# Rounded activations moved by 32 to 224 bytes against the rounded weights, in a two-layer hybrid diffusion backbone

## What is computed

```
hc = ada_ffn_half(hc, ...); hx = ada_ffn_half(hx, ...)     # SwiGLU, 1024 -> 2*2816 -> 1024
uc, ux = modulate(rms_norm(h, mix_norm[l]), shift, scale)
yc, yx = token_mixing(...)   # u @ w_in -> gated MLP | delta rule | latent attention
m = sigmoid(ga)*(ya @ w_a) + sigmoid(gb)*(yb @ w_b) + sigmoid(gc)*(yc @ w_c)
h = h + gate * (m @ w_o)
h = ada_ffn_half(h, ...)     # second SwiGLU
```

## Time and profile before

| | |
|---|---|
| runs | 2534.43 and 2532.1 us, median 2533.26 |
| profiled execution, first to last instruction | 2531.9 us |
| what lies around the span | 0.2 to 2.5 us, by the two runs |
| mean granted TensorE clock | 0.987 of full speed |
| busy PE / weight load / DVE / ACT / POOL | 2430.3 / 2061.2 / 1466.0 / 945.7 / 90.4 us |
| weights and inputs read | 306.18 MB, 121 GB/s over the span |

### The profile page before, as it was taken

One profiled execution on the slowest core, in us unless ns is written; L12 is line 12 of the kernel. 1 busy time (PEld: TensorE's weight loads), 2 busy tenths in 40 slices (PEclk: granted clock), 3 DMA queues, 4 the chain that ended last, 5 costly groups with the idle time before them and its releaser, 6 DMA issues.

```text
span 2531.9 us, 37811 instructions
## 1 busy us (share of the span) xinstructions
PE 2430.3 (96%) x15806; PEld 2061.2 (81%) x15806; DVE 1466.0 (58%) x2287; ACT 945.7 (37%) x1537; POOL 90.4 (4%) x122
## 2 busy tenths in 40 slices
PE   5999999999989999999999999999999989999999
PEld 4888877867878888888888788888886878898999
DVE  5877656355667465577655453333354667567555
ACT  2322223365554422232222232322245554444543
POOL 0000000000023000000000000000000003100000
PEclk9999999999999999999999999999999999999999
DMA  7544543201200143335454332222321220055454
GB/s 274 215 181 185 183 150 114 87 34 51 84 35 2 34 166 124 126 117 200 183 199 166 150 110 100 100 96 98 107 100 67 84 84 2 19 177 173 167 184 167
DMA packets 44663, 309.65 MB, mean 122 GB/s; under 512 B 5072, under 2 KB 6224, under 8 KB 7632
## 3 DMA queue, kind: packets, MB, share of 16 engines
q1 hardware_dynamic: 44208, 305.98, 33.5%
q10 hardware_dynamic: 288, 1.27, 0.1%
HBM read 306.18 MB, written 1.05 MB: 121 GB/s over the span
## 4 chain that ended last, share of the span: by engine, by line
PE 89%; DVE 5%; ACT 3%; issue 2%; DMA 1%; SPq 0%; POOL 0%; ACTq 0%; DVEq 0%
PE bank L1475 74%; PE bank L1841 7%; PE bank L1468 2%; PE bank L1778 1%; PE bank L1757 1%; DVE w_lo L2097 1%; DVE u_lo L2144 1%; DVE sq L2136 1%; PE bank L1506 1%; ACT w_hi L933 1%; PE bank L1691 1%; DMA mod_par<-in_mod 0%; PE bank L1518 0%; PE bank L1766 0%; ACT work L1246 0%
## 5 line engine op out<-in xcount | busy, mean ns | idle before, releaser
L2097 DVE TENSOR_TENSOR w_lo<-ring,w_hi 128x1024 fp32r<-128x1024 f32 x420 | 510.5, 1224 | 676.5 <-ACT w_hi L933 671.7
L1475 PE MATMUL bank<-u_hi,w_hi 128*128 128x512 f32 (+1 forms) x2272 | 816.7, 359 | 27.9 <-DVE w_lo L2097 14.9
L1475 PE MATMUL bank<-u_hi,w_lo 128*128 128x512 f32 (+1 forms) x2272 | 805.8, 355 | 0.0
L1475 PE MATMUL bank<-u_lo,w_hi 128*128 128x512 f32 (+1 forms) x2272 | 805.3, 354 | 0.0
L933 ACT ACTIVATE w_hi<-ring 128x1024 fp32r<-128x1024 f32 x420 | 442.9, 1059 | 837.7 <-PE bank L1475 824.1
L1475 PEld LDWEIGHTS bank<-u_hi,w_hi 128*128 128x128 f32 x2272 | 432.9, 191 | 95.6 <-issue 21.6
L1475 PEld LDWEIGHTS bank<-u_lo,w_hi 128*128 128x128 f32 x2272 | 433.0, 191 | 59.4
L1475 PEld LDWEIGHTS bank<-u_hi,w_lo 128*128 128x128 f32 x2272 | 433.3, 191 | 56.8
L1475 PE MATMUL bank<-hidden_hi,w_hi 128*128 128x512 f32 (+1 forms) x722 | 260.6, 361 | 0.0
L1475 PE MATMUL bank<-hidden_lo,w_hi 128*128 128x512 f32 (+1 forms) x722 | 259.9, 360 | 0.0
L1475 PE MATMUL bank<-hidden_hi,w_lo 128*128 128x512 f32 (+1 forms) x722 | 259.9, 360 | 0.0
(11 more groups left out here) (236 smaller groups left out, 2458.1 us busy)
## 6 DMA issues: line engine op xcount, KB each, us to landing
ring<-in_wts SPq DMA_DIRECT2D x288, 1024.0 KB, 4.8
h<-in_x SPq DMA_DIRECT2D x8, 256.0 KB, 4.1
par<-in_par ACTq DMA_DIRECT2D x2, 620.0 KB, 6.0
out<-h SPq DMA_DIRECT2D x8, 128.0 KB, 4.2
cst<-in_cst SPq DMA_DIRECT2D x1, 704.0 KB, 11.8
mod_par<-in_mod SPq DMA_DIRECT2D x1, 96.0 KB, 12.0
cond<-in_c SPq DMA_DIRECT2D x1, 8.0 KB, 1.8
```

The costliest lines, as they stand in the source:

```text
L1475: last = weights.used(pe.matmul(out, lhs[a], rhs[b], start=start and n == 0, stop=stop and n == 2))
L2097: tt(w_lo[:, b % HALVES, :], half_source(n % RING, part), w_hi[:, b % HALVES, :].bitcast(F32), ALU.subtract).then_inc(panel_left[n % RING] ...
```

## The change

The tiles u_hi, u_lo, hidden_hi, hidden_lo, m_hi and m_lo get 64 spare elements each (the arena as a whole too), and each stage reads and writes them from an offset of its own, in elements of 4 bytes. The chunks stay 2048 bytes apart. sg and ada_sum, which lie behind hidden in the arena, move up by 256 bytes. y_hi and y_lo stay, and m of layer 0 has offset 0.

```diff
+U_AT = {(0, 0): 8, (0, 1): 32, (0, 2): 16, (1, 0): 24, (1, 1): 8, (1, 2): 32}
+HIDDEN_AT = {(0, 0): 56, (0, 1): 8, (1, 0): 20, (1, 1): 56}
+MERGED_AT = (0, 8)
+SPARE = 64
...
-        u_hi = sb("u_hi", [P, DC, T], F32R)
-        u_lo = sb("u_lo", [P, DC, T], F32R)
+        u_whole_hi = sb("u_hi", [P, DC * T + SPARE], F32R)
+        u_whole_lo = sb("u_lo", [P, DC * T + SPARE], F32R)
...
-        sb("arena", [P, 48 * T])
+        sb("arena", [P, 48 * T + SPARE])
...
-        h_hi = at("hidden_hi", 0, FC, F32R)
-        h_lo = at("hidden_lo", FC, FC, F32R)
-        sg = at("sg", 2 * FC, 2)
+        h_whole_hi = nc.alloc_sbuf_tensor_at("hidden_hi", [P, FC * T + SPARE], F32R, offset=base)
+        h_whole_lo = nc.alloc_sbuf_tensor_at("hidden_lo", [P, FC * T + SPARE], F32R, offset=base + FC * SLOT)
+        sg = nc.alloc_sbuf_tensor_at("sg", [P, 2, T], F32, offset=base + 2 * FC * SLOT + 4 * SPARE)
...
-        m_hi = at("m_hi", 0, DC, F32R)
-        m_lo = at("m_lo", DC, DC, F32R)
+        m_whole_hi = nc.alloc_sbuf_tensor_at("m_hi", [P, DC * T + SPARE], F32R, offset=base)
+        m_whole_lo = nc.alloc_sbuf_tensor_at("m_lo", [P, DC * T + SPARE], F32R, offset=base + DC * SLOT)
...
+        def chunks_at(o, *wholes):
+
+            return [x[:, o:o + x.shape[1] - SPARE].rearrange("p (k t) -> p k t", t=T) for x in wholes]
+
+        def normed_chunks(l, i):
+
+            return chunks_at(U_AT[l, i], u_whole_hi, u_whole_lo)
+
+        def hidden_chunks(l, f):
+
+            return chunks_at(HIDDEN_AT[l, f], h_whole_hi, h_whole_lo)
+
+        def merged_chunks(l):
+
+            return chunks_at(MERGED_AT[l], m_whole_hi, m_whole_lo)
```

More of the change, by code:

```diff
@@ L433, in backbone @@
         base = -(-nc.sbuf_base // 32) * 32
-        sb("arena", [P, 48 * T])
+        sb("arena", [P, 48 * T + SPARE])
         def at(name, slot, n, dt=F32):
             return nc.alloc_sbuf_tensor_at(name, [P, n, T], dt, offset=base + slot * SLOT)
-        h_hi = at("hidden_hi", 0, FC, F32R)
-        h_lo = at("hidden_lo", FC, FC, F32R)
-        sg = at("sg", 2 * FC, 2)
+        h_whole_hi = nc.alloc_sbuf_tensor_at("hidden_hi", [P, FC * T + SPARE], F32R, offset=base)
+        h_whole_lo = nc.alloc_sbuf_tensor_at("hidden_lo", [P, FC * T + SPARE], F32R, offset=base + FC * SLOT)
+        sg = nc.alloc_sbuf_tensor_at("sg", [P, 2, T], F32, offset=base + 2 * FC * SLOT + 4 * SPARE)
         work = nc.alloc_sbuf_tensor_at("work", [P, 36 * T], F32, offset=base)
-        ada_sum_ffn = at("ada_sum", 46, 2)
+        ada_sum_ffn = nc.alloc_sbuf_tensor_at("ada_sum", [P, 2, T], F32, offset=base + 46 * SLOT + 4 * SPARE)
         ya, yb, yc = at("ya", 36, 4), at("yb", 40, 4), at("yc", 44, 4)
-        m_hi = at("m_hi", 0, DC, F32R)
-        m_lo = at("m_lo", DC, DC, F32R)
+        m_whole_hi = nc.alloc_sbuf_tensor_at("m_hi", [P, DC * T + SPARE], F32R, offset=base)
+        m_whole_lo = nc.alloc_sbuf_tensor_at("m_lo", [P, DC * T + SPARE], F32R, offset=base + DC * SLOT)
         def view(at, n, w=T):
@@ L937, in norm @@
             def norm(l, i, h_key):
+                u_hi, _ = normed_chunks(l, i)
                 def square(part):
@@ L977, in ffn @@
                 h0 = FC * (2 * l + f)
+                h_hi, _ = hidden_chunks(l, f)
                 def pair(i):
@@ L1345, in _ @@
                 act.wait_ge(ya_ready, l + 1)
+                m_hi, _ = merged_chunks(l)
                 for b, y in ((0, ya), (2, yc)):
@@ L1587, in second_part @@
                         spread(l, i, 1)
-                streamed([bank_of(key) for key in keys], [part_of(l, i, part)[1] for part in range(n)], u, u_rest_ready,
+                streamed([bank_of(key) for key in keys], [part_of(l, i, part)[1] for part in range(n)], normed_chunks(l, i), u_rest_ready,
                          DC * PART_AT[l, i], second_part)
-            u = (u_hi, u_lo)
             def ffn(l, f, w, carry):
+                u = normed_chunks(l, 2 * f)
                 following = (l, 1) if f == 0 else (l + 1, 0) if l + 1 < DEPTH else None
@@ L1609, in ffn @@
                         ada_sums(carry, 2 + i // 2)
-                hid = (h_hi, h_lo)
+                hid = hidden_chunks(l, f)
                 for g in range(4):
@@ L1645, in _ @@
                 ffn(l, 0, T, 0 if l == 0 else None)
+                u, merged = normed_chunks(l, 1), merged_chunks(l)
                 normed([(l, "gmu", 0), (l, "gmu", 1)], l, 1)
@@ L2031, in _ @@
                     free_bank((l, "out", c))
-                streamed([bank_of((l, "out", c)) for c in range(2)], [slice(0, w)], (m_hi, m_lo), m_rest_ready, DC * l)
+                streamed([bank_of((l, "out", c)) for c in range(2)], [slice(0, w)], merged, m_rest_ready, DC * l)
                 for p in range(1, 3):
-                    std([(l, "out", 2 * p), (l, "out", 2 * p + 1)], w, (m_hi, m_lo), None, 0)
-                std([(l, "out", 6)], w, (m_hi, m_lo), None, 0)
+                    std([(l, "out", 2 * p), (l, "out", 2 * p + 1)], w, merged, None, 0)
+                std([(l, "out", 6)], w, merged, None, 0)
                 if len(PARTS[l, 2]) > 1:
@@ L2038, in _ @@
                     free_bank((l, "out", 7))
-                    last_product((l, "out", 7), w2, (m_hi, m_lo), [(k, k, k == 0) for k in range(DC)], (l, 2))
+                    last_product((l, "out", 7), w2, merged, [(k, k, k == 0) for k in range(DC)], (l, 2))
                 else:
-                    std([(l, "out", 7)], w, (m_hi, m_lo), None, 0)
+                    std([(l, "out", 7)], w, merged, None, 0)
                     sums(l, 2, 0)
@@ L2121, in norm @@
                 items = norm_items(l, i)
+                u_hi, u_lo = normed_chunks(l, i)
                 def inverse(part):
@@ L2222, in ffn @@
                 h0 = FC * (2 * l + f)
+                h_hi, h_lo = hidden_chunks(l, f)
                 def pair(i):
@@ L2623, in _ @@
                     dve.wait_ge(out_kept[d], outs_before(l, 4, d))
+                m_hi, m_lo = merged_chunks(l)
                 def y_rest(b, y, n):
```

## The result

The changed kernel takes 2556.49 us (2555.84 to 2557.13) against 2533.26: ratio 1.0087, 95% interval 1.0058 to 1.0117. The forecast was 2471 us. The profiled execution's span is 2555.3 us, 23.4 more than before, at nearly the same mean clock (0.986, before 0.987).

A forecast was written before the change was run, and what follows sets the result against it. PE was taken as the bound, its matmul pace set by the moving tile's place. Gains of 29.9, 20.4 and 14.6 us sum to 64.9, less 3 taken back, net 62: 2533 - 62 = 2471 us, range 2430 to 2550.

The forecast's parts named there:

- that the place decides the pace: PE's matmuls of u and hidden: the moving tile's place after the weights sets the loss, 13.3 ns at 0, 20.0 at 192 (512 columns).
- the prediction's picture behind it: In PE's matmuls, reading the next stationary tile gets in the way of the moving read when both want the same memory part.
- the place has no part in it: Rival: the change does nothing to PE's pace, 2533 us; no effect, or gains and losses that cancel, had 0.14.
- I take 6.7 ns, the least loss that a one-pass matmul shows in this trace, for every place that is moved: Loss assumed per matmul at all new places of u, hidden and m; the terms gained sum to 64.9 us.
- the term of -29.9 us: u at 512 columns: 4488 matmuls each gain 6.67 ns, 29.9 us in all.
- -20.4: hidden at 512 columns: 1530 matmuls each gain 13.3 ns, 20.4 us in all.
- -14.6: u at 256 columns, moving or stationary: 2184 matmuls each gain 6.67 ns, 14.6 us in all.
- both are left by all of u and hidden: Reason for the 6.7 ns: 0 and 192, the places of the two known losses, are no longer used by u and hidden.
- the upper, 20.0 ns everywhere: Bound over all moved matmuls: the worst loss seen, 20.0 ns, at every new place, 53 us lost.
- The lower, 2 ns: Bound over all moved matmuls: only 2 ns over the columns at every new place, 106 us gained, 2427 us.
- slower: Rival: loss is high at the new places, 6.7 ns on each of u's 4488 matmuls, up to 2586 us; chance 0.14.
- The same places can hold more than one steady pace: Warning from m of layer 1 at 192, 256 columns: 117.6 ns in its streamed part where hidden has 113.3.

The follow-up runs named there:

- the 64 places: Without the model: groups of 72 three-term matmuls at places 4 bytes apart, 0 to 252; 512 columns reach 226.7 ns at six, 256 columns 113.3 at three.
- The scans: Kernels without the model: back-to-back groups of 72 three-term matmuls, each at another place; at 0 and 4 bytes 512 columns settle at 226.7 and 236.7 ns.
- worst_places: Against the kernel before, 512-column u and hidden moved to 208 bytes, the scan's slowest place: 2560.39 us, ratio 1.0107.
- two_levels: Against the kernel before, hidden at 512 columns moved to 0 bytes and u of (1,2) to 192: 2525.57 us, ratio 0.9961.
- the first two scans: Without the model: 16-byte steps up and down at four widths, then seven variants of tiles and stationary columns; mean 232.4 ns at 512 columns with 128 stationary.
- the third: Without the model: seven targets, each tried after groups at 16 different places; 512 columns at 240 bytes settled at 236.7, 233.3 or 226.7 ns.

## Why the prediction was wrong

- *What bounds the kernel, and that the place decides the pace*: right. PE is the bound, the other engines moved with it, y and m stayed, the place was shown to be the cause apart from the model, and it counts relative to the weights. How the weights' read and the moving read meet, the prediction's picture behind it, is not shown. The case against "the place has no part in it" held. The Trainium skill ("SBUF — State Buffer", "Who interferes with whom") calls TensorE's two read ports, one for the moving operand and one for the weight load, independent. The scans disagree as far as the pace goes: with DVE and ACT idle and next to no DMA, a pair of tiles 4 bytes further apart (at 4 bytes instead of 0) costs PE 10 ns a matmul.
- *The step that failed*: "I take 6.7 ns, the least loss that a one-pass matmul shows in this trace, for every place that is moved". Measured were 20.0 (at 32), 19.1 (at 128), 15.7 (at 64) and 20.0 ns (at 96) for u at 512 columns, so that the term of -29.9 us came out as 6.5 + 6.1 + 2.0 + 6.7 + 1.7 = +23.0. Hidden at 512 columns has 21.0, 20.0 and 18.4: -0.3 us for -20.4. u at 256 columns gained 2.9 and 1.4 ns where 6.7 were put: -4.6 us for -14.6. Hidden and m at 256 columns, put at 0, cost 2.6. Together +20.7 for -64.9.
- *Why it failed*: two errors in one. It took the loss at 0 (13.3) for a bad place because the trace had a lower number, but that number belonged to the other width. For 512 columns no place is better than 0, which lies 6.1 ns under the mean of the 64, and the kernel before stood there with 4488 matmuls. And it read "both are left by all of u and hidden" as a gain, when leaving a place says nothing on where one arrives. By the rows at one width alone, one place at 13.3 and one at 20.0, the fair guess for an unknown place was the mean of the two, 16.7: 4488 x 3.3 - 1530 x 3.3 is 10 us slower. The same at 256 columns (13.3 and 6.7, mean 10.0) gives 2184 x 3.3 - 828 x 3.3, 4 us faster: together 5 us slower, the right sign and not the size.
- *The bounds*: the upper, 20.0 ns everywhere, or +53 us, held as a sum, though not as a loss: hidden at 160 loses 21.0 ns, and the worst of the 64 places 26.7. The lower, 2 ns, is reached at none of the 64: the least is 13.3 ns at 512 columns and 6.7 at 256. The range ended at 2550 us since only half of "slower" was given to above 2560; the time fell in between, in the rival "slower", whose mechanism (high loss at the new places) and price (6.7 ns on u) were right, and which had 0.14. It put the turning point at a mean loss of 14.0 ns; by the stage table the mean over the 8838 moved matmuls is now 16.5, and 2.5 x 8838 is 22 us.
- *A reading*: the prediction has 283 ns for u at 256 columns from the earlier trace rows. That is gmv's row; u's own has 287. No term rests on it, since the paces were read from single matmuls.
- *"The same places can hold more than one steady pace"*: right, and it is what kept worst_places and two_levels from their sums.
- *Counts, waits, writes, clock*: as forecast. No term there is missing; DVE has 154.8 of the densest 209 us.

Left open: by what rule a place gives its pace, which of the two reads yields, if it is they that meet, and whether the PSUM bank or a longer history picks among several paces. No run has the matmuls without the weight load beside them, so a moving read quite alone wasn't seen, and the least loss of 13.3 ns at 512 columns, the same with 32 stationary columns, is not explained.

## What to carry to other kernels

In a kernel bound by back-to-back one-pass f32 matmuls, the place of the moving after the stationary tile within 256 bytes is worth 2.6% of a matmul of 512 columns from the mean place to the best, and 5.5% from the worst; it has to be measured for each moving width (here 0 bytes is best for 512 columns and 112 for 256), in a scan that reaches each place from different neighbours, so that a place with one steady pace can be chosen. When a trace shows an unknown function at two arguments, a third argument is no promise of the lower value: compare within one width, and ask whether the present place may already be the best.

## What the runs showed that was not expected

- The pace changes with every 4 bytes, repeats after 256, and has a floor above the columns' time: 226.7 ns for 213.3 at 512 columns, 173.3 for 160.0 at 384, 113.3 for 106.7 at 256.
- A steady stream of matmuls remembers what ran ahead of it: the same 72 matmuls settle at 226.7, 233.3 or 236.7 ns, at 240 bytes. The place of the group ahead doesn't settle it alone; after a group at 224 they had 233.3 ns in the first two scans and 236.6 in the third.
- A quarter of the stationary columns (32 for 128) makes the mean pace no better than 231.3 against 232.4 ns at 512 columns, and 115.8 against 118.3 at 256.
